# Two stacked blocks, one core: head norm by parts, HGRN tiles first in the output projection, x first at the opening, closing tiles with single waits

## What is computed

```python
def gated_head_norm(o, w, z):
    o = o * lax.rsqrt(jnp.mean(o * o, axis=-1, keepdims=True) + EPS)
    return o * w.astype(jnp.float32) * jax.nn.silu(z)
...
def step(s, inp):                       # GDN, over chunks
    u_n, w_n, qk_n, qg_n, kt_n, cd_n = inp
    v_new = u_n - jnp.einsum('bhcd,bhde->bhce', w_n, s)
    o = jnp.einsum('bhcd,bhde->bhce', qg_n, s) + jnp.einsum('bhcs,bhse->bhce', qk_n, v_new)
    s = s * cd_n[..., None, None] + jnp.einsum('bhcd,bhce->bhde', kt_n, v_new)
    return s, o
...
o_a = gated_head_norm(o_a, gdn_norm[i], z_gdn)
o_b = gated_head_norm(o_b, hgrn_norm[i], g_hg)
mix = jnp.concatenate([o_a, o_b], axis=-1)          # 4 + 4 heads of 128
h = h + rms_norm(mix @ w_out[i], post_mix_norm[i])
```

## Time and profile before

| | us |
|---|---|
| median of 3 runs | 1452.34 |
| lowest, highest | 1451.54, 1452.35 |
| profiled execution | 1450.62 |
| its span, first to last instruction | 1448.8 |
| PE busy in the span | 1357.2 (94%) |
| DVE, ACT, POOL busy | 886.8, 783.4, 412.0 |
| mean granted PE clock | 0.974 of full |

### The profile page before, as it was taken

One profiled execution on the slowest core, in us unless ns is written; L12 is line 12 of the kernel. 1 busy time (PEld: TensorE's weight loads), 2 busy tenths in 40 slices (PEclk: granted clock), 3 DMA queues, 4 the chain that ended last, 5 costly groups with the idle time before them and its releaser, 6 DMA issues.

```text
span 1448.8 us, 26132 instructions
## 1 busy us (share of the span) xinstructions
PE 1357.2 (94%) x8934; PEld 1235.7 (85%) x8934; DVE 886.8 (61%) x1667; ACT 783.4 (54%) x1377; POOL 412.0 (28%) x239
## 2 busy tenths in 40 slices
PE   4999958999998976899999999999999999999997
PEld 4998946999976975799999999999998888888885
DVE  3677355666567885479994255656635555555554
ACT  4645314444445733447777676676655555555553
POOL 0100301000001671007988766666650000000001
PEclk9999978999999997899999999999999999999998
DMA  6533004555544442245555544444455555555553
GB/s 233 175 118 115 30 0 155 188 188 188 190 159 146 146 146 73 102 160 170 179 188 187 176 145 135 144 146 137 141 172 186 184 185 186 187 188 188 188 184 106
DMA packets 62008, 225.16 MB, mean 155 GB/s; under 512 B 7136, under 2 KB 7520, under 8 KB 61552
## 3 DMA queue, kind: packets, MB, share of 16 engines
q1 hardware_dynamic: 59904, 217.61, 44.5%
q10 hardware_dynamic: 2032, 6.60, 1.2%
HBM read 223.13 MB, written 1.05 MB: 155 GB/s over the span
## 4 chain that ended last, share of the span: by engine, by line
PE 88%; DVE 5%; POOL 2%; ACT 2%; issue 2%; DMA 1%; ACTq 0%; POOLq 0%; DVEq 0%
PE bank L497 76%; PE bank L920 4%; POOL arena L1440 1%; DVE arena L1842 1%; PE bank L520 1%; PE bank L570 1%; PE bank L691 1%; PE bank L477 1%; ACT arena L973 1%; PE bank L701 1%; PE bank L699 1%; DMA arena<-in_meta 1%; ACT w_hi L1003 1%; PE bank L713 1%; PE bank L873 0%
## 5 line engine op out<-in xcount | busy, mean ns | idle before, releaser
L1003 ACT ACTIVATE w_hi<-ring 128x1024 fp32r<-128x1024 f32 x414 | 438.7, 1060 | 516.6 <-PE bank L497 342.2
L1513 DVE TENSOR_TENSOR w_lo<-ring,w_hi 128x1024 fp32r<-128x1024 f32 x274 | 338.3, 1235 | 311.9 <-ACT w_hi L1003 305.5
L497 PE MATMUL bank<-hT_hi,w_hi 128*128 128x256 f32 (+2 forms) x1728 | 432.4, 288 | 3.6 <-DVE hT_lo L1505 1.4
L497 PE MATMUL bank<-hT_lo,w_hi 128*128 128x256 f32 (+2 forms) x1728 | 424.1, 283 | 0.0
L1467 POOL TENSOR_TENSOR w_lo<-ring,w_hi 128x1024 fp32r<-128x1024 f32 x128 | 310.5, 2428 | 172.9 <-ACT w_hi L1003 172.7
L497 PEld LDWEIGHTS bank<-hT_hi,w_hi 128*128 128x128 f32 x1728 | 328.0, 190 | 7.0 <-issue 2.9
L497 PEld LDWEIGHTS bank<-hT_lo,w_hi 128*128 128x128 f32 x1728 | 328.9, 190 | 0.1
L497 PE MATMUL bank<-hT_hi,w_lo 128*128 128x256 f32 (+2 forms) x1728 | 240.7, 282 | 5.7 <-POOL w_lo L1449 5.7
L497 PEld LDWEIGHTS bank<-hT_hi,w_lo 128*128 128x128 f32 x1728 | 221.2, 190 | 6.1 <-POOL w_lo L1449 6.1
L497 PE MATMUL bank<-w_hi,wgt_hi 128*128 128x512 f32 x504 | 200.0, 397 | 0.0
L497 PE MATMUL bank<-w_hi,wgt_lo 128*128 128x512 f32 x504 | 199.8, 396 | 0.0
(11 more groups left out here) (318 smaller groups left out, 1598.7 us busy)
## 6 DMA issues: line engine op xcount, KB each, us to landing
ring<-in_stream SPq DMA_DIRECT2D x414, 512.0 KB, 3.2
arena<-in_rows ACTq DMA_DIRECT2D x1, 1536.0 KB, 17.4
consts<-in_consts ACTq DMA_DIRECT2D x1, 1152.0 KB, 12.5
h<-in_x ACTq DMA_DIRECT2D x1, 1024.0 KB, 7.4
arena<-in_keys ACTq DMA_DIRECT2D x1, 1024.0 KB, 4.7
arena<-in_rows ACTq DMA_DIRECT2D x1, 512.0 KB, 3.6
out_h<-arena SPq DMA_DIRECT2D x2, 256.0 KB, 2.1
out_h<-arena ACTq DMA_DIRECT2D x2, 256.0 KB, 2.5
```

What stands on the lines that cost most here:

```text
L497: mm = nc.tensor.matmul(o, a, b, start=first and not low_part and xp is x[0], stop=last and low_part)
L1003: nc.scalar.activation(w_hi[:, g % S, :], ring[:, g % R, :], ACT.Copy).then_inc(hi_done, 1)
L1513: nc.vector.tensor_tensor(w_lo[:, g % S, :], ring[:, g % R, :], w_hi[:, g % S, :].bitcast(F32), ALU.subtract).then_inc(lo_done, 1)
```

## The change

1. **Opening.** x comes in two halves of 128 tokens, the first of all DMAs on ACT's queue and on SP's. `cols`, the meta rows, `wab` and `small` move to SP's queue, the large pieces of `consts` and `rows` to after the first blocks. A one-column Square brings ACT's table load forward. ACT squares each half as it lands; tiles 0 and 1 are split later. The meta rows' transposes move from the start to behind tile 8, their copy on DVE to behind the third convolution block. -1/2 is set by a memset on POOL.
2. **Head norm by parts.** ACT squares and sums the HGRN heads in levels 3 and 4 (a square per head and token half, with the sum accumulated), POOL makes their factors behind its mask of level 5, and DVE scales and gates them ahead of level 6. The GDN gates are multiplied by the q and k factors in levels 1 and 2. q of chunk 1 is multiplied by exp of its decay (`qgain`, from ACT), so that PE adds both terms of chunk 1's output in banks 4 and 5, which it opens with zero matmuls. Squares, factors and gating of the GDN heads go by chunk, from PSUM.
3. **Output projection.** Its tiles come in the order 4 to 7, 0 to 3, so HGRN blocks first. Their transposes stand inside the scan; those of the GDN blocks behind the second tile. The sums go to banks 0 to 3, and the zero matmuls for the MLP's sums (`open_sums`) now stand behind `transposes(2)`.
4. **Closings.** Each closing tile waits for its own split and operand, where it is used.

The squares moved ahead of both splits of tiles, and the meta rows' square behind them. The diff's core:

```diff
@@ SP, opening
-            for s in range(R):
+            sp_eng.dma_start(h[:, 1, :], rows_of_x(1)).then_inc(x_loaded[1], 16)
+            sp_eng.dma_start(cols[:, :], cols_in).then_inc(front_in, 16)
+            for s in range(2):
                 sp_eng.dma_start(ring[:, s, :], stream_in[s]).then_inc(slot_full[s], 16)
+            sp_eng.dma_start(meta_raw[0:META, :], meta_in).then_inc(meta_in_sb, 16)
...
@@ PE
             def closing_rows(tiles, b0, first=False, halves_done=True):
                 for t in range(NT):
-                    for j, ((slot, low), lhs) in enumerate(tiles):
+                    for j, (g, lhs, ready) in enumerate(tiles):
+                        slot = g % S
+                        pe.wait_ge(hi_done, g + 1)
+                        if ready:
+                            pe.wait_ge(*ready)
...
-            heads(4, lambda hd: conv_c(0, 2 * hd + 1), hcol(state)).then_inc(ks_full, 1)
+            pe.wait_ge(q_scaled, 1)
+            for hd in range(NH):
+                nc.tensor.matmul(second_rows(hd), conv_c(0, 2 * hd + 1), state[:, hd * P:(hd + 1) * P],
+                                 start=False, stop=False)
...
+            pe.wait_ge(hgrn_gated, 8)
+            out_transposes(OUT_ORDER[:4])
             pe.wait_ge(r_ready, 2)
             heads(0, lambda hd: yinv[:, 2 * hd + 1, :], hcol(rhs[:, 1, :])).then_inc(vn_full, 1)
             pe.wait_ge(vn_out, 2)
...
-            transposes(1)
-            rows_out(G_OUT, 8, hT_lhs, 4, stage=1)
+            pe.wait_ge(gdn_gated, 4)
+            for j in range(6):
+                hT_block(1, j)
+                row_tile(tile(G_OUT + j), lambda t: out_lhs(j, t), 0, j == 0, False)
+                if j == 1:
+                    pe.wait_ge(gdn_gated, 8)
+                    out_transposes(OUT_ORDER[4:])
+            hT_block(1, KD - 1)
+            closing_rows([(G_OUT + j, [out_lhs(j, t) for t in range(NT)], None) for j in (6, 7)], 0)
...
+            transposes(2)
             open_sums()
-            transposes(2)
@@ ACT, levels and scan
+                elif l <= 2 * NT:
+                    t = l - NT - 1
+                    for hd in range(NH):
+                        nc.scalar.activation(normed[...], osb[:, t, NH + hd, :], ACT.Square, accum_out=hsum[...])
...
+            act.wait_ge(oa_full, 1)
             for hd in range(NH):
+                head_square(bank[1][:, hd * P:(hd + 1) * P], hd, cc(rqs, 2 * hd))
+            out_blocks(0)
+            for hd in range(NH):
+                if hd % 2 == 0:
+                    act.wait_ge(oa_full, 2 + hd // 2)
+                head_square(bank[4 + hd // 2][...], NH + hd, cc(rqs, 2 * hd + 1))
+            his(G_OUT, 2)
+            out_blocks(1)
+            his(G_OUT + 2, 4)
@@ POOL
+                if l == LEVELS - 2:
+                    head_factors(8, 8, 8)
+            head_factors(0, NH, 12)
+            head_factors(NH, NH, 16)
@@ DVE
+            nc.vector.tensor_tensor(conv[:, 0:NH, P:T], conv[:, 0:NH, P:T], qgain, ALU.mult).then_inc(q_scaled, 1)
...
+                if l == LEVELS - 1:
+                    dve.wait_ge(hr_done, 1)
+                    hgrn_rows(0)
+                    hgrn_rows(1)
```

More of the change, by code:

```diff
@@ L947, in _ @@
                 row_tile(w, lambda t: wgt_lhs(n, t), 0, False, False)
[L948 to L950 removed]
+            closing_rows([(G_V + n, [wgt_lhs(n, t) for t in range(NT)], (wgt_out, n + 1))
+                          for n in (N_KEYS - 2, N_KEYS - 1)], 0)
         @block.scalar
@@ L1092, in _ @@
             act.wait_ge(grow_full, 1)
+            for b in range(2):
+                nc.scalar.activation(qgain[:, 2 * b:2 * b + 2, :],
+                                     bank[2 + b][:, :].rearrange("p (h t n) -> p h t n", h=2, t=NT)[:, :, 1, :], ACT.Exp)\
+                    .then_inc(qgain_out, 1)
             for hd in range(NH):
```

231 lines of the change are left out of this document (135 added, 96 removed).

## The result

| | before | after |
|---|---|---|
| median of runs on the same chip, us | 1451.94 | 1414.86 |
| ratio, 95% interval | | 0.9746, 0.9734 to 0.9759 |
| profiled execution, its span | 1450.6, 1448.8 | 1414.5, 1412.7 |
| PE busy in the span, us | 1357.2 | 1349.1 |
| PE idle in the span, us | 91.6 | 63.6 |

37.1 us less. Between the profiled executions the forecast took 29.0 off 1450.6, which is 1421.6; the profile after has 1414.5, 7.1 less. The rest is that the median lies 0.3 above the profiled execution here, where the forecast carried over 1.7.

What follows compares the result with a forecast made beforehand. PE was taken as the bound, busy nearly all the span, so only its idle time could return. Terms -10.2 - 15.7 + 0.4 - 0.75 - 2.7 = -29.0 gave 1421.6 profiled, median 1423 us, range 1418 to 1431.

Steps and rivals of the forecast that it cites:

- The opening: Start to first tile matmul: x lands at 5.7, first tile matmul at 12.6 instead of 23.89; -10.2 with margins and transposes.
- The meta rows' transposes: Moved behind tile 8, they still cost PE some 0.7 us at full clock.
- The inverse: Its levels hide all the added work; the last mask ends 1.7 us before PE wants it.
- The last closing: Final closing: six of 24 matmuls run in the 1.95 us wait, leaving 0.5 and less half clock; -2.7 us.
- the rivals: x not faster, 0.10; dearer ACT, POOL, DVE handshakes, 0.12; PE staying at half clock, 0.02; ring starved, 0.06.
- (d): Rival: the opening's late DMAs starve the ring, two late tiles cost 4 us, time 1427; chance 0.06.
- Scan and head norm: First output tile at 195.65 instead of 212.07, -16.4; late transposes +1.1, closing -0.4; sum -15.7 us.
- MLP's start: Zero matmuls between third transposes and first tile cost +0.3 to +1.3, earlier clock rise up to 1.7 back; taken +0.4 us.
- Closings of the MLP and the gate: Each closing loses its recorded wait of 0.38 us; -0.75 together.

Runs made afterwards that it cites:

- e6: Changed kernel with both halves of x on ACT's queue, SP's beginning with cols and ring tile 0; 1419.2 us (0.9785).
- e4: Kernel before with only the closing tiles waiting one by one, each for its own split and operand; 1446.0 us (0.9966).
- e2: Kernel before with only the new opening; 1437.4 us (0.9907).
- e9: Kernel before with the -1/2 columns in a buffer of their own, so consts is sixteen columns shorter; 1449.0 us beside 1450.5 (0.9983).
- e17: Kernel before with an unused 64-byte buffer ahead of wgt_hi; 1447.4 us beside 1451.7 (0.9975).
- e7: Changed kernel with the large late DMAs of consts and rows issued ahead of ACT's squares; 1416.6 us (0.9763).
- e14: The changed kernel, unchanged, measured and profiled again; 1416.6 us beside 1450.5 (0.9764).
- e3: Kernel before with only the new head norm, output tile order and place of the zero matmuls; 1432.7 us (0.9872).
- e16: Changed kernel with the four zero matmuls for the MLP's sums moved back ahead of the third transposes; 1415.8 us (0.9759).
- e12: Changed kernel with 22 unused zero matmuls in PE's idle 6.15 us ahead of the third transposes; 1417.1 us (0.9773).
- e13: Changed kernel with unused zero matmuls at five waits of PE, the 13.5 us wait's 40 standing behind it; 1421.6 us (0.9803).
- e15: Changed kernel with unused zero matmuls in five idle gaps of PE, 52 of them ahead of the 13.5 us wait; 1410.8 us (0.9719).
- e19: Changed kernel with the 16 one-column products that sum the squares of q and k made 64 wide; 1414.5 us (0.9747).
- e20: Changed kernel with both the zero matmuls of e15 and the 64-column sums of e19; 1407.6 us (0.9704).
- e1: The kernel before, unchanged, profiled once more; 1452.5 us (one run).

## Why the prediction was right and wrong

**Right.** The reading of PE's waits as the list of what can be gained: idle time fell by 28.0 us, and 25.9 of it are the four waits named in the earlier trace rows. (Of the rest, 1.5 is a wait for POOL's `w_lo` in the second block, 4.0 before and 2.5 after, which nothing in the change aimed at.) The opening (where the DMA engines of the kernel before were not "busy all the time", as the prediction says, but 0.59 over the first 5 us and 1.02 over the next, which changes nothing in its sum): x forecast at 5.7, measured 5.66; `ident` 8.3, measured 8.8; first tile matmul 12.6, measured 12.84; at the scan -10.2 forecast, -10.25 measured. That this last fits so closely is luck: both first profiles had the short stretch of 3.4 us behind the narrow products, and from the second profile of before to that of the changed kernel it is -8.5. The meta rows' transposes moved and not gone: segment +0.8, forecast 0.7 and 0.4 of margins. That x lands later with a ring tile beside it, at equal shares with the ring (e6: 8.1, measured 7.96). The inverse hides all its new work: the last mask ends at 163.99 and PE wants it at 166.74, 2.75 of slack against 1.7 forecast. The last closing: -2.7, measured -2.99, with the clock at full behind a wait of 0.55. Of this 1.4 is the wait and 1.5 the stretch behind it, and e4, which changes the closings alone, gives both (15.71 to 12.79). But e2, e9 and e17 lack the stretch with the old closing too: with the buffers where the changed kernel has them, the closing by itself gives only 1.4 (14.16 in e2 to 12.72). None of the rivals came true, and e7 shows that (d) had ample room.

**Wrong, by step.** The sum is 7.1 us short in the profiles. What failed is that it took PE's speed while busy as given: the half clock in the scan was carried over, its shortening at the MLP's start put at nothing, and the tiles of the expert layer left out. These three are 1.5, 1.5 and 1.4 us; terms of the head norm set too high are 1.3, and waits of closings set too low and scatter of the clock in the second block most of the rest.

- *Scan and head norm, -15.7, measured -18.48.* Up to the first output tile -16.4 was forecast, and 28.55 us from the scan's first product became 9.91, -18.6. With both at half clock in the scan (before and the changed kernel again) it is 28.55 to 11.53, -17.0; with both at full (e4 or e17 and after) 27.11 to 9.91, -17.2. So 1.5 us are the stretch that before had and after had not, which the prediction carried over as if it were part of the scan ("all is as before"). Another 0.7 are terms set too high: chunk 1's values 0.7 later, measured 0.35 (10.27 to 10.62 from the scan's first product to its last, e14); the last product 1.2, measured 0.92 to the next instruction. From the first tile to the third transposes +0.7 was forecast and 0.16 measured (29.35 to 29.51): the late transposes cost 0.79 (188.82 to the next tile at 189.61) and not 1.1, and the closing gave 0.5, not the 0.36 of its wait.
- *MLP's start, +0.4, measured -0.98 from the third transposes to the second tile (9.17 to 8.19).* The zero matmuls cost 0.5, as forecast. But the first tile takes 3.37 us and not 4.84 (217.51 to 220.88), since the half clock ended 0.7 us into it. e3, with the old closings, has 7.91 from transposes to second tile, so this is not the closings' doing. The prediction knew this term, "up to 1.7 back", and put it at nothing. The half clock behind the wait lasted 10.2 us in five of six profiles with the old code and 6.8 in all of the new that have no fillers. Why, stays open: e16 moved the zero matmuls back and it was 6.8 still, and e4 had 3.4 with the old code.
- *Closings of the MLP and the gate, -0.38 each, measured -0.66 and -0.62.* The recorded idle time ahead of a closing was taken as what it costs; from like point to like point it cost more.
- *Second block up to the experts, beside the gate's closing 0, measured -0.7.* It lies between the fifth and the sixth transposes and scatters with the clock: from the MLP's end to the sixth transposes it is 167.7 to 168.7 in six profiles with the old closings and 166.5 to 167.5 in eight with the new and no fillers there, of which the closing explains 0.62.
- *Expert layer, 0, measured -1.43.* A moved buffer, which the prediction didn't look at (e9, e17): a tile takes 2.800 us and not 2.811.
- *The range.* It was made of bounds for the steps, without the scatter of the clock. The second profiled execution of the changed kernel is 5.0 us longer than the first, nearly all by stretches, and of before 1.9, so even a right sum would have needed 2 to 3 us more at both ends. With the second measurement (1416.6) the miss would have been 1.4 below the range, with the first 3.1.

## What to carry to other kernels

Split a time difference into PE's idle time, its work lost at half clock and its work at full clock before looking for causes; here the three were 28.0, 6.5 and 1.6 us, and the forecast had the first and, of the second, only the 1.5 behind the last wait. Profile the same kernel twice before reading a stretch at half clock as a property of its code. Work without use in a gap paid here where PE came last behind it, and only when it stood ahead of the wait and not behind (e12, e13, e15). Products of one column are worth trying wider where they take as long (e19, e20).

## What the runs showed of the hardware

- Products of one column and of 64 take the same time (3.68 and 3.73 us for 16), but PE at full clock fell to half within or right behind the first in all fifteen profiles that have them, and at the second in none of three.
- Stretches at half clock behind the same instructions differ in length between executions: 3.4 us in before and 6.8 in e1, and 3.4 in after and 10.2 in e14, behind the products of one column; 3.4 and none in the scan (before and e4). They are found at narrow products and short gaps (0.8 us ahead of the scan's products) as well as behind long waits.
- 64 bytes more or less in the place of the operand of PE's products change a tile of 12 products of 512 columns from 2.811 to 2.800 us (before and e1 against e9 and e17), the same in every profile.
- Two small pieces of `consts` (128x256 and 128x145), issued behind x on its queue, were there 3.7 us after x's second half with ring tiles beside them (e6), and 3.1 us after x in the changed kernel.
- POOL's power took 1.64 us for eight columns and 1.01 for four, ACT's square of 128 columns with its sum 0.29 from one to the next, from PSUM 0.34; the prediction had estimated 1.7, 1.0 and 0.5.
